# A second fold of the squares of q and k, one pass with two blocks of ones, and a two-pass low-rank product in a hybrid GLA and dilated-attention encoder layer

## The reference, cut to what matters

```
h = rms_norm(x);  z = h @ w_in            # columns: GLA q, k, v, gate, low-rank decay (2 x 16), attention q, k, v, merge gates
la_f = log_sigmoid(z_low_f @ wa2_f + ba_f) / 16        # the same backward: the low-rank decay
qa = rms_norm(q_attention, qnorm_g);  ka = rms_norm(k_attention, knorm_g)   # per head, over 128 channels
# dilated attention: 3 groups (window, dilation) x 4 heads on qa, ka, v; groups combined by their softmax denominators
```

## Time and profile before

| | |
|---|---|
| median of 3 runs | 2613.53 us (2613.05 to 2615.77) |
| profiled execution | 2613.04 us, span 2611.5 us |
| mean granted TensorE clock | 0.999 of full speed (2.4 GHz) |
| TensorE busy, share of span | 2574.7 us, 99% |
| VectorE busy | 1465.4 us, 56% |
| ScalarE busy | 1094.2 us, 42% |
| GpSimd busy | 245.2 us, 9% |
| attention units | 12, in the first half of the span |

### The profile page before, as it was taken

One profiled execution on the slowest core, in us unless ns is written; L12 is line 12 of the kernel. 1 busy time (PEld: TensorE's weight loads), 2 busy tenths in 40 slices (PEclk: granted clock), 3 DMA queues, 4 the chain that ended last, 5 costly groups with the idle time before them and its releaser, 6 DMA issues.

```text
span 2611.5 us, 40206 instructions
## 1 busy us (share of the span) xinstructions
PE 2574.7 (99%) x15350; PEld 2336.4 (89%) x15350; DVE 1465.4 (56%) x2224; ACT 1094.2 (42%) x1784; POOL 245.2 (9%) x407
## 2 busy tenths in 40 slices
PE   7999999999999999999999999999999999999998
PEld 6888888888888898888888888899999999999887
DVE  4435543454443634336443353988888877677843
ACT  4554345542554425544353333633333433333621
POOL 3000000100001000010010011011111210000000
PEclk9999999999999999999999999999999999999999
DMA  3132122221222212122163233144344763442021
GB/s 116 25 34 64 53 66 29 38 66 43 74 33 27 81 37 72 25 34 73 45 245 109 96 115 113 65 140 144 134 135 145 281 214 101 163 148 81 25 73 57
DMA packets 201705, 236.42 MB, mean 91 GB/s; under 512 B 14928, under 2 KB 172176, under 8 KB 201520
## 3 DMA queue, kind: packets, MB, share of 16 engines
q0 software_dynamic: 34576, 138.78, 16.5%
q1 hardware_dynamic: 164864, 95.05, 13.5%
q10 hardware_dynamic: 2080, 0.14, 0.1%
HBM read 168.73 MB, written 65.02 MB: 90 GB/s over the span
## 4 chain that ended last, share of the span: by engine, by line
PE 95%; DVE 2%; issue 1%; ACT 1%; DMA 0%; POOL 0%; POOLq 0%; ACTq 0%; DVEq 0%; SPq 0%
PE banks L1085 18%; PE banks L1087 18%; PE banks L1086 18%; PE banks L1441 5%; PE banks L1443 5%; PE banks L1442 5%; PE banks L1370 5%; PE banks L1372 5%; PE banks L1371 5%; PE banks L1198 2%; PE banks L1179 1%; PE banks L1280 1%; PE banks L1267 1%; PE banks L1189 1%; PE banks L1241 1%
## 5 line engine op out<-in xcount | busy, mean ns | idle before, releaser
L1085 PE MATMUL banks<-act_hi,w_hi 128*128 128x512 f32 (+1 forms) x2424 | 903.1, 373 | 0.7 <-DVE act_lo L2075 0.7
L1087 PE MATMUL banks<-act_hi,w_lo 128*128 128x512 f32 (+1 forms) x2424 | 860.3, 355 | 0.0
L1086 PE MATMUL banks<-act_lo,w_hi 128*128 128x512 f32 (+1 forms) x2424 | 858.9, 354 | 0.0
L1087 PEld LDWEIGHTS banks<-act_hi,w_lo 128*128 128x128 f32 x2424 | 457.2, 189 | 66.2
L1085 PEld LDWEIGHTS banks<-act_hi,w_hi 128*128 128x128 f32 x2424 | 458.4, 189 | 58.4 <-DVE act_lo L2075 0.9
L1086 PEld LDWEIGHTS banks<-act_lo,w_hi 128*128 128x128 f32 x2424 | 459.3, 189 | 53.8
L1721 ACT ACTIVATE work<-banks 128x512 f32<-128x512 f32 (+4 forms) x228 | 113.8, 504 | 412.3 <-PE banks L1087 412.3
L1441 PE MATMUL banks<-op,ring 128*128 128x320 f32 x896 | 277.4, 310 | 3.1 <-DVE ring L2596 1.6
L1442 PE MATMUL banks<-op,ring 128*128 128x320 f32 x896 | 276.9, 309 | 0.0
L1443 PE MATMUL banks<-op,ring 128*128 128x320 f32 x896 | 276.9, 309 | 0.0
L2050 DVE TENSOR_TENSOR w_lo<-w_raw,w_hi 128x1024 fp32r<-128x1024 f32 (+1 forms) x111 | 131.5, 1184 | 128.9 <-ACT w_hi L1525 127.3
(11 more groups left out here) (347 smaller groups left out, 4146.8 us busy)
## 6 DMA issues: line engine op xcount, KB each, us to landing
w_raw<-in_w_in_dram SPq DMA_DIRECT2D x76, 512.0 KB
operand_scratch<-work POOLq DMA_DIRECT2D x112, 320.0 KB, 2.8
op_f<-operand_scratch POOLq DMA_DIRECT2D x28, 1280.0 KB, 6.4
w_raw<-in_w_mlp_dram SPq DMA_DIRECT2D x48, 512.0 KB, 5.3
work<-gate_scratch POOLq DMA_DIRECT2D x16, 640.0 KB, 5.5
gate_scratch<-work POOLq DMA_DIRECT2D x15, 640.0 KB, 3.3
raw<-in_w_mlp_dram SPq DMA_DIRECT2D x16, 512.0 KB, 5.7
work<-weight_scratch POOLq DMA_DIRECT2D x12, 640.0 KB, 6.0
```

The lines of the kernel that those rows point to most:

```text
L1085: nc.tensor.matmul(out, wh, rh, start=first and k == 0, stop=False, skip_group_check=True)
L1086: nc.tensor.matmul(out, wh, rl, start=False, stop=False, skip_group_check=True)
L1087: mm = nc.tensor.matmul(out, wl, rh, start=False, stop=k == kt - 1, skip_group_check=True)
```

## The change

- The squares of k and of q are each folded once more, from 64 to 32 partitions (VectorE, directly behind the first fold). The high part of k goes to partitions 0 to 31 of `sq_parts` and its low part to 32 to 63, those of q to 64 to 95 and 96 to 127. ScalarE's rounding moves to -31 and -15, VectorE's subtraction to -28 and -12.
- One pass at -9 with `halves_r`, two 64x64 blocks of ones on the diagonal and zeros elsewhere, gives the sums of k in partitions 0 to 63 and those of q in 64 to 127. One Ln group and one Exp at -7 follow.
- At -3 VectorE multiplies k and q in halves of 64 partitions, four instructions in place of two.
- `halves_r` lies in memory that `state` uses later, so VectorE writes it anew at the start of each head, four small instructions.
- T_BLOCK goes from 6 to 11 and T_CW from 264 to 269, T_STAT with T_BLOCK. The ticks of the V transposes and copies, T_COMBINE and all GLA ticks stay.
- The low-rank columns move to columns 32 to 63 of their slab, their low part to 64 to 95 beside them. One pass of columns 32 to 95 over act_hi and one of columns 0 to 63 over act_lo make two passes per k-tile; ScalarE copies rows 32 to 63 to SBUF, VectorE adds rows 0 to 31, and the two copies and the subtraction into `lowrank` read the sum.

```diff
@@ -191,6 +191,7 @@
         ident = small("ident", [P, P])
         ones_r = small("ones_r", [P, P], FR)
         ones = ones_r[:].bitcast(F32)
+        halves_r = at("halves_r", [P, P], FR, shared + 5632)
         mask_b = small("mask_b", [P, P], U8)
         r_bc = at("r_bc", [P, T], F32, pos[0])
         x_next_r = at("x_next_r", [P, T], FR, shared)
@@ -448,12 +449,12 @@
 
 
 
-        T_BLOCK, BSTEP = 6, 4
+        T_BLOCK, BSTEP = 11, 4
         T_WA2 = 100
         T_STAT = T_BLOCK + BSTEP * BLK
         T_LR, T_Y, T_ABS, T_EXP, T_LN = (268, 275), (272, 280), (274, 282), (277, 285), 286
         T_SCAN, T_DECAY, T_QK, T_KEND = (292, 313), (314, 328), (328, 335), 341
-        T_CW, T_COMBINE = 264, 283
+        T_CW, T_COMBINE = 269, 283
         T_VT, T_VN = (322, 325, 330, 334, 337), (327, 328, 334, 340, 341)
         T_GLA, GSTEP = 352, 6
         T_OUT = T_GLA + GSTEP * NT
@@ -1115,7 +1116,13 @@
                     if c == 0:
                         pe.wait_ge(primed, 1)
                         pe.wait_ge(w_split, 2)
-                mm = steps(0, c, k0, k1, KT, act_hi, act_lo)
+                t0, tw = CHUNKS[c]
+                out = bank[c][0:64, 0:tw]
+                for k in range(k0, k1):
+                    nc.tensor.matmul(out, w_hi[:, 0, k * P + 32:k * P + 96], act_hi[:, k, t0:t0 + tw],
+                                     start=k == 0, stop=False, skip_group_check=True)
+                    mm = nc.tensor.matmul(out, w_hi[:, 0, k * P:k * P + 64], act_lo[:, k, t0:t0 + tw],
+                                          start=False, stop=k == KT - 1, skip_group_check=True)
                 if k1 == KT:
                     mm.then_inc(mm_done, 1)
 
@@ -1139,18 +1146,14 @@
 
                 u = 3 * h + g
                 kz, qz, vz = (z[:, (3 * (g % 2)) + i, :] for i in range(3))
-                if tau in (-22, -10):
-                    e = int(tau == -10)
-                    pe.wait_ge(sq_low, 2 * u + e + 2)
-                    if e == 0:
-                        if g == 0:
-                            pe.wait_ge(head_done, h + 1)
-                        pe.wait_ge(stt_read, 2 * h + g + 1)
-                        pe.wait_ge(max_done, 10 * u + 1)
-                    else:
-                        pe.wait_ge(ln_done, 2 * u + 2)
+                if tau == -9:
+                    pe.wait_ge(sq_low, 2 * u + 3)
+                    if g == 0:
+                        pe.wait_ge(head_done, h + 1)
+                    pe.wait_ge(stt_read, 2 * h + g + 1)
+                    pe.wait_ge(max_done, 10 * u + 1)
                     for c, (t0, tw) in enumerate(CHUNKS):
-                        mm = nc.tensor.matmul(bank[(3, 4, 7)[c]][:, 0:tw], ones_r[:], sq_parts[:, e, t0:t0 + tw],
+                        mm = nc.tensor.matmul(bank[(3, 4, 7)[c]][:, 0:tw], halves_r[:], sq_parts[:, 0, t0:t0 + tw],
                                               start=True, stop=True)
                     mm.then_inc(ss_done, 1)
                 if tau in (4, 5, 9):
@@ -1529,7 +1532,7 @@
 
 
             lr = w_raw[:].rearrange("p (k n) -> p k n", n=P)
-            act.dma_start(lr[:, :, 0:2 * RANK], w_in[:, :, C_LR:C_LR + 2 * RANK]).then_inc(w_loaded, 32)
+            act.dma_start(lr[:, :, 32:64], w_in[:, :, C_LR:C_LR + 2 * RANK]).then_inc(w_loaded, 32)
             act.dma_start(g_mix[:], a["norm_mix_g"].rearrange("(k p) -> p k", p=P)).then_inc(g_mix_loaded, 16)
 
             done = []
@@ -1553,7 +1556,7 @@
             act.wait_ge(g_mix_loaded, 16)
             x_highs(0, 0, 4)
             act.wait_ge(primed, 1)
-            act.wait_ge(w_zero, 1)
+            act.wait_ge(w_zero, 2)
             act.wait_ge(w_loaded, 32)
             A(w_hi[:, 0, :], w_raw[:], ACT.Copy).then_inc(w_high, 1)
             squares(8, 6)
@@ -1565,8 +1568,12 @@
             act.wait_ge(const_dma, 80)
             for c, (t0, tw) in enumerate(CHUNKS):
                 act.wait_ge(mm_done, c + 2)
+                if c == 0:
+                    act.wait_ge(x_sumsq, 7)
+                A(ar[0:32, 2, t0:t0 + tw], bank[c][32:64, 0:tw], ACT.Copy).then_inc(lr_high, 1)
+                act.wait_ge(x_norm, NT + c + 1)
                 for r0 in (0, 64):
-                    A(lowrank[r0:r0 + 32, t0:t0 + tw], bank[c][0:32, 0:tw], ACT.Copy).then_inc(lr_high, 1)
+                    A(lowrank[r0:r0 + 32, t0:t0 + tw], ar[0:32, 3, t0:t0 + tw], ACT.Copy).then_inc(lr_high, 1)
             act.wait_ge(evac, 4)
 
 
@@ -1584,20 +1591,16 @@
                     act.wait_ge(qk_ready, 2 * u + 1)
                     act.wait_ge(sq_low, 2 * u + e + 1)
                     A(ar[:, 11, :], (kz, qz)[e], ACT.Square).then_inc(sq_made, 1)
-                if tau in (-34, -17):
-                    e = int(tau == -17)
-                    act.wait_ge(sq_folded, 2 * u + e + 2)
-                    A(sq_parts[0:64, e, :], ar[0:64, 11, :], ACT.Copy).then_inc(sq_ready, 1)
-                if tau in (-18, -8):
-                    e = int(tau == -8)
-                    act.wait_ge(ss_done, 2 * u + e + 2)
+                if tau in (-31, -15):
+                    e = int(tau == -15)
+                    act.wait_ge(sq_folded, 4 * u + 2 * e + 3)
+                    A(sq_parts[64 * e:64 * e + 32, 0, :], ar[0:32, 11, :], ACT.Copy).then_inc(sq_ready, 1)
+                if tau == -7:
+                    act.wait_ge(ss_done, u + 2)
                     for c, (t0, tw) in enumerate(CHUNKS):
-                        ins = A(ar[:, e, t0:t0 + tw], bank[(3, 4, 7)[c]][:, 0:tw], ACT.Ln, bias=eps[:], scale=1.0 / P)
-                    ins.then_inc(ln_done, 1)
-                if tau == -7:
-                    act.wait_ge(ln_done, 2 * u + 3)
-                    for e in range(2):
-                        A(ar[:, e, :], ar[:, e, :], ACT.Exp, scale=-0.5).then_inc(r_ready, 1)
+                        A(ar[:, 1, t0:t0 + tw], bank[(3, 4, 7)[c]][:, 0:tw], ACT.Ln, bias=eps[:], scale=1.0 / P).then_inc(ln_done, 1)
+                    act.wait_ge(ln_done, 3 * u + 4)
+                    A(ar[:, 1, :], ar[:, 1, :], ACT.Exp, scale=-0.5).then_inc(r_ready, 1)
                 b, at_ = divmod(tau - T_BLOCK - 2, BSTEP)
                 if at_ == 0 and 0 <= b < BLK:
                     act.wait_ge(max_done, 10 * u + b + 2)
@@ -2053,7 +2056,9 @@
             def chunk_done(n, c):
                 dve.wait_ge(mm_done, slab_chunks(n) + c + 2)
 
-            v_.memset(w_raw[:].rearrange("p (k n) -> p k n", n=P)[:, :, 2 * RANK:P], 0.0).then_inc(w_zero, 1)
+            lr = w_raw[:].rearrange("p (k n) -> p k n", n=P)
+            v_.memset(lr[:, :, 0:32], 0.0).then_inc(w_zero, 1)
+            v_.memset(lr[:, :, 64:P], 0.0).then_inc(w_zero, 1)
 
             def squares(t, before):
                 dve.wait_ge(x_loaded[t], 16)
@@ -2083,7 +2088,10 @@
             normed_x(2)
             x_lows(0, 0, 4)
             dve.wait_ge(primed, 1)
-            split_low(0, 0)
+            lr_w = w_hi[:, 0, :].rearrange("p (k n) -> p k n", n=P)
+            dve.wait_ge(w_high, 2)
+            v_.tensor_tensor(lr_w[:, :, 64:96], lr[:, :, 32:64], lr_w[:, :, 32:64].bitcast(F32), ALU.subtract
+                             ).then_inc(w_split, 1)
             normed_x(3)
             x_lows(0, 4, KT)
             squares(9, 2)
@@ -2099,8 +2107,13 @@
             dve.wait_ge(const_dma, 80)
             v_.tensor_scalar(g_k[:], g_k[:], -(P ** -0.5), None, ALU.mult).then_inc(const_dve, 1)
             for c, (t0, tw) in enumerate(CHUNKS):
-                dve.wait_ge(lr_high, 2 * c + 2)
-                v_.tensor_tensor(lowrank[32:64, t0:t0 + tw], bank[c][0:32, 0:tw], lowrank[0:32, t0:t0 + tw].bitcast(F32),
+                dve.wait_ge(lr_high, 3 * c + 1)
+                if c == 0:
+                    dve.wait_ge(x_sumsq_d, 3)
+                v_.tensor_tensor(ar[0:32, 3, t0:t0 + tw], bank[c][0:32, 0:tw], ar[0:32, 2, t0:t0 + tw], ALU.add
+                                 ).then_inc(x_norm, 1)
+                dve.wait_ge(lr_high, 3 * c + 3)
+                v_.tensor_tensor(lowrank[32:64, t0:t0 + tw], ar[0:32, 3, t0:t0 + tw], lowrank[0:32, t0:t0 + tw].bitcast(F32),
                                  ALU.subtract).then_inc(evac, 1)
 
 
@@ -2113,11 +2126,13 @@
                     e = int(tau == -20)
                     dve.wait_ge(sq_made, 2 * u + e + 2)
                     v_.tensor_tensor(ar[0:64, 11, :], ar[0:64, 11, :], ar[64:P, 11, :], ALU.add).then_inc(sq_folded, 1)
-                if tau in (-31, -14):
-                    e = int(tau == -14)
+                    dve.wait_ge(sq_folded, 4 * u + 2 * e + 2)
+                    v_.tensor_tensor(ar[0:32, 11, :], ar[0:32, 11, :], ar[32:64, 11, :], ALU.add).then_inc(sq_folded, 1)
+                if tau in (-28, -12):
+                    e = int(tau == -12)
                     dve.wait_ge(sq_ready, 2 * u + e + 2)
-                    v_.tensor_tensor(sq_parts[64:P, e, :], ar[0:64, 11, :], sq_parts[0:64, e, :].bitcast(F32), ALU.subtract
```

(20 more changed lines are left out.)

## The result

The changed kernel takes **2664.02 us** (median of 4 runs, 2661.43 to 2666.63) against 2614.65 for the kernel before (4 runs, 2613.05 to 2616.55): ratio **1.0188, interval 1.0176 to 1.0200**. It is slower, as forecast, but by 49 us where 35 were forecast, and above the range (2628 to 2657). The profiled execution took 2662.88 with a span of 2661.3, 49.8 more than the span before; its mean granted clock is 0.992 (before: 0.999).

The account below looks back on a forecast made before the run. TensorE was taken to bound the kernel, busy 99% of the span. From 2613.04 us, the terms -6.8 - 2.9 + 36 + 6 + 3 = +35.3 gave 2648 us, with a range of 2628 to 2657.

Parts of the forecast that it names:

- Who waits behind it: TensorE's third V transpose at tick 9 waits 3.0 us for VectorE's V copy, twelve units: +36 us.
- What bounds the kernel: TensorE, busy 99% of the span, no listed waits in head loops; a pass saved there is worth its whole pitch.
- Ones pass: Attention units: each of twelve loses one set of three matmuls, 0.57 us: -6.8 us.
- Low-rank product: Opening: 8 of 24 passes fewer, main loop starts at 41.8 instead of 44.65: -2.9 us, bounds -3.75 and -1.5.
- Ln table load in the path: ScalarE's statistics: the only Ln group's table load now delays the roots; load to first Exp 1.30 us, no drain.
- Half products: VectorE's normalisation: four 64-partition products, 1.55 us each (1.47 if overlapping, 1.58 with gap), 6.2 us against 2.94.
- rival 2: VectorE's normalisation: half the partitions at half the price, no wait at the V transposes, 2606 us; chance 0.06.
- The wait's size: Tick 9, first unit: V copy ends at 98.11, TensorE comes at 95.19, wait 3.0 us.
- Second folds: Ticks 35 and 52: folds of 1.49 us on VectorE delay block output copies TensorE needs: +6 us, bounds 0 and +9.
- Rival 3: Attention blocks: each fold also delays max, exp and transposes, costing 24 us in place of 6, 2666; chance 0.08.
- Combination weights: Ticks 264 to 269: weights 1.7 us later, first GLA product waits 1.5 in head 1: +3 us, bounds 0 and +6.
- Nothing for `halves_r`: Head start: four VectorE steps, about 1 us, cost nothing ahead of a weight split due 22 ticks later.

Follow-up runs that it names:

- Experiments 1: Changed kernel with the third V transposes moved from tick 9 to 14 and their copy from 10 to 15: 2609.25 us, ratio 0.9978 against the kernel before.
- experiment 5: Changed kernel with third V transposes at 14, their copy at 15, and eight unawaited semaphore increments ahead of VectorE's head loop: 2607.59 us, ratio 0.9968.
- experiment 4: Kernel before with the low-rank edit alone: 2610.07 us, ratio 0.9983.
- experiment 2: Changed kernel with a one-column Ln at tick -11, loading the Ln table ahead of the chunk's copy: 2634.43 us, ratio 1.0074 against the kernel before.
- experiment 7: Kernel before with each product of k and q in two halves of 64 partitions, nothing else: 2658.97 us, ratio 1.0171.

## Why the prediction was off

**The step that failed** is "Who waits behind it": it takes the wait at tick 9 as 3.0 us of standing still and multiplies by 12. The wait itself was right, 38.5 against 36. What the step left out is what a standstill leaves behind on TensorE: the passes after it run at half clock, 15.3 us over nine units. With that term the sum would have been 50.6. That this is close to the 49.8 measured is partly luck, since the smaller errors cancel: folds and combine were 7.9 us too high; the wait 2.5 too low, and the weight split (2.4) and the MLP stage (3.0) stood at nothing. The profile before had a hint, one row, read only as harmless: the 3.02 us standstill in the MLP; its execution happened to run on at full clock, and the prediction asked of no wait what clock stood behind it.

Point by point:

- *What bounds the kernel*: right. A pass taken from TensorE in the heads is worth its pitch: in the first unit of each head, where the ones pass of k stood (tick 50) with nothing else moved, TensorE is 0.57 us quicker than before. Experiments 1 and 5 are faster once little or nothing waits, though by less than the sum of the passes (Open, below).
- *Ones pass*: right, -6.8 by 36 matmuls fewer at the pitch of the earlier trace rows.
- *Low-rank product*: right in mechanism, -3.5 against -2.9 (experiment 4: -3.46).
- *Ln table load in the path*: right; experiment 2 prices it at 1.4 us per unit against 1.3. The Trainium skill ("ScalarE: Activation LUTs", What ACT_TABLE_LOAD costs) adds a drain of 1380 ns to the load; the rows have the load 0.02 us behind the copies, Ln 1.29 us after the load's start, and no drain. The Trainium skill ("ScalarE: Activation LUTs", Table sets: the hidden batching unit) has Ln followed by Exp under one load; the trace doesn't agree, each unit has two.
- *Half products*: the upper value was right, 1.57 us apart against the 1.55 taken. This refutes rival 2 (experiment 7: halves alone cost 1.7%). The Trainium skill ("VectorE: DVE Perf Modes", Two Vector instructions with no wait between them) holds an instruction that starts in another quadrant (a group of 32 partitions) than the one ahead until that one has finished. The trace agrees: each of the four starts on other partitions than the one ahead, and the pitch of 1.57 is no shorter than the 1.55 that one takes.
- *The wait's size*: the sum for the first unit left out that TensorE has lost the ones pass of k at -22 as well, 0.57 us, on both sides of the race: the chunk's copy came 1.1 us earlier against the loop's start, not 0.57, and TensorE reached tick 9 earlier by the same 0.57. The two cancel. The remaining 0.2 is 0.1 in the statistics and 0.1 in the products.
- *Second folds*: mis-sized, +6 against 1.1. The fold itself cost what was said, the folds lie 1.5 us apart:

```profile
129.49 1.49 DVE L2128 TENSOR_TENSOR work<-work 64x1280 f32<-64x1280 f32 x1 [0.86 <-ACT work L1593]
131.01 1.48 DVE L2130 TENSOR_TENSOR work<-work 32x1280 f32<-32x1280 f32 x1
132.42 0.27 DVE L2184 COPY work<-banks 128x128 f32<-128x128 f32 x1
```

But the Square ahead of them started at 128.19, 1.5 us after tick 48 (126.71), not 2.4, so the copy was done at 132.69 and TensorE came for it at 133.35. Only the count around tick 44 held in part, 0.3 us in the second unit of each head (forecast 0.4) and nothing in the first (forecast 0.1). Rival 3 is refuted.
- *Combination weights*: no cost in this execution. The weights were ready 1.5 us later against tick 283, near the 1.7 said, but from their last step to the combine it took 11.2 to 11.6 us, where it had taken 12.7 and 13.1 in the two heads whose combine waited and 12.1 in the others. In head 1 VectorE's last step before the first GLA product ended at 621.20, with TensorE at 621.41 and no wait. That is luck of the execution in part: with the same ticks, head 2 of experiment 5 took 12.5 from the last step to the combine, which waited 1.7, and the head took 0.8 longer than the others.
- *Nothing for `halves_r`*: wrong in the changed kernel, by 2.4 us. The four steps put the split 0.65 us later, and the cover named for them, a weight split due 22 ticks later, was used up by VectorE's longer standstill at the loop's top. TensorE waited for that split at tick 24 of heads 1 to 3. It takes both: experiment 4 has the standstill alone, experiment 5 the steps alone. The step of the prediction looked only at what the change adds inside the loop.

**Open:** the kernel of experiment 5 gains 3.6 us in its heads where the ones pass gives 6.8. The waits behind the folds take 1.1, and 0.8 lies around the first GLA product of head 2, where the weights came late; some 1.3 us are not assigned. What beside the length of a standstill decides whether half clock follows isn't shown. A kernel with full-width products and correct scaling (r of k and q both on 128 partitions) was not tried.

## What to carry to other kernels

Price a wait on TensorE in two parts, the standstill and the passes after it: here a wait of 3.2 us cost 4.3 to 4.5 on average, and moving its consumer until nothing waited (five ticks) turned a loss of 1.9% into a gain of 0.2%. When blocks are moved in a hand-written order, look also at the steps that stay behind: here the third V transposes kept their tick while what they wait for came later. And a VectorE instruction split by partitions took twice the time here: two halves of 64 partitions 3.11 us, one of 128 partitions 1.54.

## What the runs showed of the hardware

- At or behind a standstill of TensorE of 1.8 to 3.2 us the granted clock fell to half (1.2 GHz) in some cases: in the heads for 3.41 us each time, with full clock after it. Over twelve like waits each it was 0 of 12 at 0.7 us, 1 at 1.8, 8 at 2.5, 9 at 3.2; the same 3.02 us wait in the same kernel did it in two executions of three.
- VectorE stood for about 3.0 us or about 6 us (5.6 to 6.4) at the top of its loop from the second pass on, depending on what lies ahead of the loop.
- A VectorE instruction on 64 or 32 partitions took as long as one on 128 (1.49 and 1.48 us for the folds of 1280 elements).
- In this kernel an Ln table load and an Exp table load stood in every unit, 1.28 us each, with no further gap behind them.
